# Output projections by seven quadrant products: two products accumulated in place, the additions into x in another order

## The reference, cut to what matters

```python
# first block, odd layer (retention), and second block, both layers
x = x + m_lat[2] * y_lat                  # y_lat = (gated retention output) @ odd_w_out,  2048 -> 1024
x = x + gt1 * (merged @ w_o[l])           # 1024 -> 1024, l = 0, 1
# behind each of them: norm, and a feed-forward
h = rms_norm_2(x, norm_ffn[l]) * (1.0 + sc2) + sh2
x = x + gt2 * ((silu(up_act) * up_lin) @ w_down[l])
```

## Time and profile before

| what | us |
|---|---|
| median of three runs | 2651.59 (2650.97 to 2651.84) |
| the profiled execution, its own time | 2649.23 |
| its span | 2647.4 |
| PE busy | 2549.9 (96%) |
| PE weight loads busy | 1940.2 (73%) |
| DVE busy | 1584.4 (60%) |
| ACT busy | 648.0 (24%) |
| granted TensorE clock, mean over the span | 0.996 |

### The profile page before, as it was taken

The page is one execution under the profiler, slowest core; times in us unless marked ns, Lnnn a source line. Parts: engine busy times, 40 slices in busy tenths (PEclk is TensorE's granted clock), DMA queues, the critical chain, the costliest instruction groups (busy, mean ns, idle before and its releaser), DMA issues.

```text
span 2647.4 us, 39241 instructions
## 1 busy us (share of the span) xinstructions
PE 2549.9 (96%) x15996; PEld 1940.2 (73%) x15996; DVE 1584.4 (60%) x3133; ACT 648.0 (24%) x1717; POOL 0.2 (0%) x4
## 2 busy tenths in 40 slices
PE   6999899999999999999999999999999999999999
PEld 2545557888887864599996845668997854667999
DVE  4856667655877543266664664447773764437785
ACT  3144412111002111122202152233321144232320
POOL 0000000000000000000000000000000000000000
PEclk9999999999999999999999999999999999999999
DMA  8531115555574684245643432134663433114563
GB/s 334 194 95 44 45 32 169 153 175 171 201 276 160 256 301 173 80 128 160 191 165 127 159 64 96 65 112 137 167 198 132 148 101 96 65 66 143 164 178 122
DMA packets 339375, 386.66 MB, mean 146 GB/s; under 512 B 11116, under 2 KB 272380, under 8 KB 326908
## 3 DMA queue, kind: packets, MB, share of 16 engines
q1 hardware_dynamic: 336460, 378.15, 44.3%
q10 hardware_dynamic: 2736, 6.01, 0.6%
HBM read 383.08 MB, written 1.05 MB: 145 GB/s over the span
## 4 chain that ended last, share of the span: by engine, by line
PE 76%; DVE 12%; DMA 5%; issue 4%; ACT 3%; SPq 0%; ACTq 0%; DVEq 0%
PE acc L865 28%; PE mx L865 12%; PE acc L916 9%; PE acc L904 7%; PE acc L930 6%; DMA mod_w<-in_w_ada 2%; DVE arena L2514 2%; DMA mod_w<-in_mod_w 2%; PE acc L1285 2%; PE acc L1234 1%; PE mx L1633 1%; DVE arena L3356 1%; DVE hT L2547 1%; PE mx L1095 1%; PE mx L1620 1%
## 5 line engine op out<-in xcount | busy, mean ns | idle before, releaser
L865 PE MATMUL acc<-arena 128*128 128x128 f32 (+1 forms) x2312 | 369.4, 302 | 3.5 <-DVE arena L3102 1.0
L865 PEld LDWEIGHTS acc<-arena 128*128 128x128 f32 x2312 | 321.9, 191 | 22.2 <-ACT gate L2184 1.4
L2514 DVE SCALAR_TENSOR_TENSOR arena<-mod_w,vcols,arena 128x2048 f32<-128x2048 f32 x98 | 228.4, 2348 | 71.7 <-DMA mod_w<-in_w_ada 58.2
L904 PE MATMUL acc<-ring,hT 128*128 128x512 f32 x576 | 251.2, 596 | 5.9 <-ACT hT L1935 4.6
L916 PE MATMUL acc<-hT,ring 128*128 128x256 f32 (+1 forms) x1024 | 249.7, 406 | 0.8 <-DVE arena L3134 0.8
L930 PE MATMUL acc<-ring,hT 128*128 128x512 f32 x512 | 247.6, 605 | 0.7 <-ACT hT L1967 0.7
L916 PEld LDWEIGHTS acc<-hT,ring 128*128 128x128 f32 x1024 | 194.0, 190 | 55.0 <-issue 32.1
L904 PEld LDWEIGHTS acc<-ring,hT 128*128 128x128 f32 x576 | 109.3, 191 | 144.4 <-issue 139.3
L865 PE MATMUL acc<-hT,ring 128*128 128x128 f32 (+1 forms) x1336 | 202.7, 301 | 3.9 <-ACT hT L1935 1.7
L2878 DVE TENSOR_TENSOR arena<-ring 128x512 f32<-128x512 f32 (+1 forms) x136 | 91.7, 674 | 191.0 <-PE acc L865 182.1
L865 PE MATMUL acc<-arena,ring 128*128 128x128 f32 (+1 forms) x1288 | 199.0, 297 | 2.3 <-DVE x L2935 1.7
(11 more groups left out here) (433 smaller groups left out, 3414.4 us busy)
## 6 DMA issues: line engine op xcount, KB each, us to landing
ring<-in_w_in SPq DMA_DIRECT2D x28, 2048.0 KB
mod_w<-in_w_ada SPq DMA_DIRECT2D x48, 1024.0 KB, 5.3
ring<-in_ffn_w_in SPq DMA_DIRECT2D x88, 512.0 KB
ring<-in_w_up SPq DMA_DIRECT2D x88, 512.0 KB
mod_w<-in_mod_w SPq DMA_DIRECT2D x40, 1024.0 KB, 4.9
ring<-in_odd_w_in SPq DMA_DIRECT2D x12, 2048.0 KB
ring<-in_ffn_w_out SPq DMA_DIRECT2D x16, 1024.0 KB
ring<-in_w_down SPq DMA_DIRECT2D x16, 1024.0 KB
```

The source lines that it names most:

```text
L865: ins = nc.tensor.matmul(out, w[:, k, :], h[:, k, :], start=start and k == 0, stop=stop and k == n - 1, skip_group_check=more)
L904: ins = nc.tensor.matmul(b[:, 0:width], src[:, k, P * i:P * (i + 1)], w[:, k, :], start=k == 0, stop=k == KD - 1)
L2514: ins = V.scalar_tensor_tensor(acc_, mod_w[:, i % 2, :], vcols[:, at:at + 1], acc_, ALU.mult, ALU.add)
```

## The change

In the three projections, product 2 is accumulated onto product 1's bank once ACT has copied product 1 out, and product 3 onto product 5's bank once DVE has added product 5 into `x`. PE's order in a pair becomes 1, 4, 2, 5, 6, 7, 3. Products 1 and 5 alternate between two banks by pair. DVE runs a new function `quadrant_added` with seven gated additions and two sums a pair in place of nine and two. In `added_to_x`, which the feed-forwards keep, two additions into quadrant (1, 0) stand ahead of u3; the counts that PE and ACT wait for are renumbered to the new places. In `w_o` three of the four weight sums of pair 1 move from behind the fourth merge job to behind the third; of the first four weight sums of the feed-forward one stays ahead of the additions of pair 3, and three go behind them, ahead of `scaled_x`.

```diff
-WHERE = {1: 6, 2: 4, 4: 3, 5: 0, 6: 5, 7: 1, 3: 2}
+WHERE = {1: (6, 0), 4: (3, 3), 5: (4, 2), 6: (5, 5), 7: (1, 1)}
...
+                    t, e, d, first = tile.n, 28 * u + 7 * (p - 1), 28 * u + 7 * p, p == 0
...
+                    if p >= 2:
+                        pe.wait_ge(out_e, e - 7 + 2)
                     product(where[1], a_[0][0], b_[0][0], True, True, evens if first else lambda k: None).then_inc(out_d, 1)
 
-                    if p:
+                    if first:
+                        odds(pairs - 1)
+                    else:
                         pe.wait_ge(out_e, e + 1)
-                    product(where[2], a_[0][1], b_[1][0], True, True, odds if first else lambda k: None).then_inc(out_d, 1)
-
                     pe.wait_ge(out_ws, 4 * u + p + 1)
-                    if p:
-                        pe.wait_ge(out_e, e + 2)
                     product(where[4], s4, b_[1][1], True, True).then_inc(out_d, 1)
+
+                    pe.wait_ge(out_dt, 4 * u + p + 1)
+                    product(where[1], a_[0][1], b_[1][0], False, True, more=True).then_inc(out_d, 1)
...
                     if first:
                         pe.wait_ge(out_ts, 4 * u + 4)
-                    else:
-                        pe.wait_ge(out_e, e + 7)
-                    product(where[3], a_[1][1], t4, True, True).then_inc(out_d, 1)
+                    pe.wait_ge(out_e, d + 3)
+                    product(where[5], a_[1][1], t4, False, True, more=True).then_inc(out_d, 1)
```

In `added_to_x` (the old order of its tail was u3, (0,1), (1,1), (1,0) with product 5, (1,0) with u2, (1,0) with product 3):

```diff
                 V.tensor_tensor(u2, where[6], t1, ALU.add).then_inc(sem_e, 1)
-                dve.wait_ge(sem_e, e + 3)
+                gated(1, 0, where[5]).then_inc(sem_e, 1)
+                dve.wait_ge(sem_e, e + 4)
+                link(gated(1, 0, u2))
                 dve.wait_ge(full, d + 6)
                 V.tensor_tensor(u3, where[7], u2, ALU.add).then_inc(sem_e, 1)
-                dve.wait_ge(sem_e, e + 4)
+                dve.wait_ge(sem_e, e + 5)
                 gated(0, 1, u3).then_inc(sem_e, 1)
                 gated(1, 1, u3)
-                gated(1, 0, where[5]).then_inc(sem_e, 1)
-                dve.wait_ge(sem_e, e + 6)
-                link(gated(1, 0, u2))
                 dve.wait_ge(full, d + 7)
                 gated(1, 0, where[3]).then_inc(sem_e, 1)
```

In the merge loop and the call for `w_o`:

```diff
-                    if n >= 2:
-                        out_weights_summed("w_o", n - 2, 4)
+                    if n == 2:
+                        out_weights_summed("w_o", 0, 4)
+                        out_weights_summed("w_o", 1, 4, (0, 1, 2))
+                out_weights_summed("w_o", 1, 4, (3,))
                 job_done("mergeT", KD)
                 quadrants("w_o", 4 + 2 * l, hT[:, :, 0:256], 4, 2,
-                          lambda: weights_summed((KF + 12) * (2 + l), pl.tile[f"up@{l}"], 4))
+                          lambda: weights_summed((KF + 12) * (2 + l), pl.tile[f"up@{l}"], 4, (0,)),
+                          lambda: weights_summed((KF + 12) * (2 + l), pl.tile[f"up@{l}"], 4, (1, 2, 3)))
```

More of the change, by code:

```diff
@@ L958, in quadrants @@
                 b_, (t2, t3, t4) = out_blocks(src), out_input_sums(pairs)
-                where = {n: seven(WHERE[n], P) for n in WHERE}
                 stage(name)
                 for p in range(4):
-                    t, e, first = tile.n, 28 * u + 7 * (p - 1), p == 0
+                    where = {n: seven(WHERE[n][p % 2], P) for n in WHERE}
+                    t, e, d, first = tile.n, 28 * u + 7 * (p - 1), 28 * u + 7 * p, p == 0
                     if pairs == 8:
@@ L991, in quadrants @@
                     else:
-                        pe.wait_ge(out_e, e + 3)
+                        pe.wait_ge(out_e, e + 4)
                     product(where[6], s2, t2, True, True).then_inc(out_d, 1)
                     if p:
-                        pe.wait_ge(out_e, e + 4)
+                        pe.wait_ge(out_e, e + 5)
                     product(where[7], s3, t3, True, True).then_inc(out_d, 1)
@@ L1471, in seven_products @@
                         if p:
-                            pe.wait_ge(st_e, before + 6)
+                            pe.wait_ge(st_e, before + 4)
                         else:
@@ L1491, in seven_products @@
                         if p:
-                            pe.wait_ge(st_e, before + 4)
+                            pe.wait_ge(st_e, before + 5)
                         else:
@@ L2217, in ready @@
                         if p:
-                            act.wait_ge(out_e, 28 * u + 7 * p - 4)
-                        nc.scalar.activation(out_temps(pairs)[0], seven(WHERE[1], P), ACT.Copy).then_inc(out_dt, 1)
-                    act.wait_ge(out_e, 28 * u + 7 * p + (7 if block % 2 else 5))
+                            act.wait_ge(out_e, 28 * u + 7 * p - 3)
+                        nc.scalar.activation(out_temps(pairs)[0], seven(WHERE[1][p % 2], P), ACT.Copy).then_inc(out_dt, 1)
+                    act.wait_ge(out_e, 28 * u + 7 * p + (7 if block % 2 else 6))
                 return ready
@@ L2239, in down0_done @@
                         mod_turn()
-                act.wait_ge(st_e, 7 * p + (7 if block % 2 else 5))
+                act.wait_ge(st_e, 7 * p + (7 if block % 2 else 6))
             squares(2, both, down0_done)
@@ L2864, in _, with weights_summed @@
                     residual_part(PARTS.index(slot - 1))
-            def weights_summed(n, tile, pairs):
+            def weights_summed(n, tile, pairs, only=(0, 1, 2, 3)):
                 s2, s3, s4 = weight_sums(n, pairs)
                 f, m = divmod(n, KF + 12)
[L2869 to L2875, removed]
+                if 0 in only:
+                    if m >= 2:
+                        kind, count = ("down" if pl.released[tile - 2][0] == "down" else "part", pl.released[tile - 2][1])
+                        if m < KF + 2:
+                            dve.wait_ge(st_x, KF * f + m - 1)
+                        else:
+                            dve.wait_ge(st_d if kind == "down" else w_part, count)
+                    dve.wait_ge(h_in[tile % (2 * RING)], pl.landed[tile][1])
                 w = half_tile(tile, 2 * pairs)
                 a00, a01, a10, a11 = (w[:, :, e, P * i:P * (i + 1)] for i in range(2) for e in range(2))
[L2878 to L2881, removed]
+                if 0 in only:
+                    V.tensor_tensor(s3, a11, a10, ALU.subtract)
+                if 1 in only:
+                    link(V.tensor_tensor(a10, a10, a00, ALU.subtract))
+                if 2 in only:
+                    link(V.tensor_tensor(s2, a11, a10, ALU.subtract))
+                if 3 in only:
+                    V.tensor_tensor(s4, a01, s2, ALU.subtract).then_inc(st_ws, 1)
             def out_weights_summed(name, p, pairs, only=(0, 1, 2, 3)):
@@ L2961, in added_to_x, with gated, quadrants @@
                         add_square(use + 1, block, width)
-            def quadrants(name, use, src, pairs, summed, early):
-                u, where = OUT_USE[name_of(name)], {n: seven(WHERE[n], P) for n in WHERE}
+            def quadrant_added(use, p, where, temps, d, n):
+                t1, u2, u3 = temps
+                first, m = 16 + 24 * (use % 2), mb[:, use // 2 % 2]
+                def gated(i, t, y):
+                    at = x[:, 1, 2 * p + i, P * t:P * (t + 1)]
+                    return V.scalar_tensor_tensor(at, y, m[:, 0, first + 2 * p + i:first + 2 * p + i + 1], at, ALU.mult, ALU.add)
+                dve.wait_ge(out_d, d + 2)
[13 more added lines that the diff above has]
+                gated(0, 1, u3).then_inc(out_e, 1)
+                gated(1, 1, u3)
+                dve.wait_ge(out_d, d + 7)
+                gated(1, 0, where[5]).then_inc(out_e, 1)
+                for block in (2 * p, 2 * p + 1):
+                    if 0 < block < KD - 1:
+                        add_square(use + 1, block, 256)
+            def quadrants(name, use, src, pairs, summed, early, late=None):
+                u = OUT_USE[name_of(name)]
                 inputs_summed(4 * u, out_blocks(src), out_input_sums(pairs), summed=out_ts)
@@ L2971, in quadrants @@
                         early()
-                    added_to_x(use, 256, p, where, out_temps(pairs), (out_d, 28 * u + 7 * p), (out_dt, 4 * u + p),
-                               (out_e, 28 * u + 7 * p))
+                    quadrant_added(use, p, {n: seven(WHERE[n][p % 2], P) for n in WHERE}, out_temps(pairs),
+                                   28 * u + 7 * p, 4 * u + p)
+                if late:
+                    late()
                 scaled_x(use + 1, 256)
```

9 lines of the change are left out of this document (4 added, 5 removed).

## The result

| | median us | runs | lowest to highest |
|---|---|---|---|
| before | 2650.74 | 11 | 2648.19 to 2652.06 |
| changed | 2658.39 | 11 | 2654.60 to 2660.91 |

The ratio is 1.0028, with a 95% interval of 1.0019 to 1.0037: the changed kernel is slower by 7.4 us (7.65 between the medians). The forecast was +3.4 and "within 0.2%"; the result is beyond that line by a little, outside the 2651 to 2656.9 that the forecast took for itself, inside the whole range (by 0.1 us), and beside rival B's 2659.2. The profiled execution took 2655.66 (span 2653.9, mean granted clock 0.997), 6.4 more than that of before.

What follows compares the result with a forecast made beforehand. The prediction took PE as the bound (76% of the chain, DVE 12%). w_o -5.07, ret_out +7.76 and down projections -1.11 gave +1.6; one clock fall, +1.8, made +3.4, so 2655.0 us, range 2648.0 to 2658.5.

Steps and rivals of the forecast that it cites:

- rival B: ret_out: the clock falls after both stalls, 3.0 us each, +7.6 in all, 2659.2 us; chance 0.14.
- `w_o`, the tail: End of w_o: DVE no longer late, scaling 3.19 us after the last product; gains 2.66 and 3.67 us.
- The start: w_o, pair 0: third product waits for ACT's copy of product 1, +0.63 us in each layer.
- Pairs 1 and 2, moved sums: w_o: the new wait for DVE's third addition and the weight sums moved ahead of the merge job cost 0.
- `ret_out`, the stall: ret_out: product 3 waits for DVE's third addition by 1.11, 3.26 and 3.39 us in pairs 0 to 2, +7.76.
- The clock: ret_out: two stalls may each bring half clock at about even chance; one fall taken, +1.8 us.
- Rivals A and C: A: PE doesn't stall in ret_out, -6.2 us, chance 0.12. C: DVE remains the bound in w_o, +6.0 us, 0.08.
- Down projections: Last addition of the kernel 0.77 us earlier, 0.17 less in each of two middle ones; sum -1.11 us.

Runs made afterwards that it cites:

- experiment 7: Changed kernel with DVE's first three additions ahead of the next pair's weight sums in ret_out, and ACT's table load ahead of mergeT's copies: 0.9974 of before, 2643.79 us.
- experiment 4: Changed kernel plus three 128x512 constant matmuls into an unused bank ahead of the wait in pairs 1 and 2 of ret_out: 1.0016 of before, 2655.61 us.
- experiment 2: Changed kernel with DVE's first three additions of a pair in ret_out ahead of the next pair's weight sums: 0.9983 of before, 2647.75 us.
- experiment 9: The changed kernel itself, profiled once more: one run, 2657.07 us.
- experiment 1: Changed kernel with ret_out back on seven banks and the old order of products: 0.9976 of before, 2645.08 us.
- experiment 6: Kernel before with only added_to_x's new order of additions, all projections on seven banks in the old order of products: 0.9985 of before, 2646.63 us.

## Why the prediction was nearly right

**`w_o`, the tail: right.** Scaling 3.19 after the last product was predicted; measured 1814.62 - (1810.59 + 0.89) = 3.14. The three late weight sums are hidden by 0.19, as the scaling still waits for ACT; the clock doesn't fall. **The start: right.** 1.53 - 0.89 = 0.64 against 0.63, and experiment 7 shows the cause. **Pairs 1 and 2, moved sums: right**, no wait shows. Together -1.92 - 2.92 = -4.84 in the stages, against -5.07.

**`ret_out`, the stall: right in place and cause, 0.9 too small.** Without a fall of the clock (experiment 4) the delays are 1.20, 3.58, 3.80 and 0.10, 8.68 in all against 7.76. The 0.9 comes in every pair. I took the additions' place from the old rows and let PE go on at full pace, but the product after a wait starts with an instruction longer than in a dense run (2.02 or 2.05 against 1.95), and since the tile's load is released by product 3, that tenth enters the loop again, once a pair. The rest is the load: from the end of product 3 to the first weight sum it took 7.99 in pair 1 and 8.11 in pair 2 before (the first from 1138.79 + 1.95 to 1148.73), and 8.23 and 8.43 in experiment 4. Why it took longer is open. Experiment 2 shows the cause: with the additions ahead of the sums the term is 0.

**The clock: the step that was mis-sized.** "Two stalls at about even chance: I take one, +1.8". Of eight long waits in four executions seven were followed by 0.50, so two falls are usual. That is rival B's mechanism. Its price of 3.0 a fall was too high, however: against the 8.68 without a fall, one fall cost 1.5 and two cost 2.8, 2.2 and 4.1, 1.1 to 2.0 each. So B's mechanism held while its sum, which comes within 1 us of the median, owes that partly to luck: too much for the clock stands against 0.9 too little for the loop and 1 to 2 us outside the stages (below). Nor was it more than luck that the median stayed inside the range: four of the eleven runs lie above its end at 2658.5. Slow products behind product 3 of pair 1 cost nothing, because pair 2 waits anyway: its idle is 3.23 in experiment 9, where product 3 alone was slow, and 2.15 in the first profile, where the next one took 2.97. Only product 3 itself lies in the loop; after the second fall the slow products of pair 3 count too, for that pair has no wait to absorb them.

**Rivals A and C: refuted.** PE stands in three pairs of `ret_out`, and in `w_o` neither an addition of pairs 1 and 2 nor a late sum holds anything up. A's gain of 6.2 is what the rest of the change is worth without the stall: 6.4 in experiment 1, 4.5 (2.1 to 6.9) in experiment 2.

**Down projections: right in kind, smaller.** -0.54 at the end instead of -0.77. The last addition did move by 0.77 against u3, as forecast: it starts 0.86 behind it and not 1.63. But u3 itself now starts 0.50 after the start of product 3 instead of 0.27, because the two additions into (1, 0) stand ahead of it; that takes 0.23 back, and the prediction left it out. The rows, before and after:

```profile
2641.53 0.29 DVE L2950 TENSOR_TENSOR hT<-acc,hT 128x128 f32<-128x128 f32 x1 [0.45 <-PE acc L865]
2648.77 0.29 DVE L2958 TENSOR_TENSOR hT<-acc,hT 128x128 f32<-128x128 f32 x1
2649.63 0.34 DVE L2941 SCALAR_TENSOR_TENSOR x<-acc,mb,x 128x128 f32<-128x128 f32 x1
```

The 0.17 waits in the two middle ones are gone.

**The sum.** The retention stage takes 363.85, 365.10 and 363.99 in the three profiles of the changed kernel, 10.8 to 12.1 more than before. So -4.84 - 0.54 + 10.8 to 12.1 = +5.5 to +6.7. Between the profiled executions themselves (2655.66, 2657.07 and 2657.04 against 2649.23) it is +6.4, +7.8 and +7.8, and between the medians +7.65: 1 to 2 us lie outside these stages. Feed-forward 1 holds 1.35, 1.28 and 1.58 of them. In the first of the three PE waited there for its first down tile (0.53) and for the sums on it (0.93). But the kernel with `ret_out` as before shows the same (215.73), and so does the one with `w_o` alone changed (215.93), while the one with `ret_out` as before and the table moved doesn't (214.40). So this varies between executions, and no run here says how often in which kernel, nor whether the change has a part in it. The filler kernel has 217.14. The stretch from the kernel's first scaling to its second varies too, and within one kernel: 362.83, 364.39 and 365.16 in the three profiles of the changed one, 364.57 in that of before. Both are open.

## What to carry to other kernels

When an accumulation goes onto a bank that was just read, the wait moves from "a pair later" to "the same pair", and everything that stands in the reader's list ahead of that read can move onto the path. Put the read first, and the work for the next tile behind it: that order was worth about 11 us here, and with it accumulating onto the read bank cost nothing in `ret_out` that these runs can tell. In `w_o` the same holds for ACT: a table load ahead of its copy cost 0.6 to 0.7 us a layer until it was moved. Before adding a wait, follow it once around: if the waiting work itself frees the buffer whose load stands ahead of the wait, the period becomes the sum of the loop (16.3 instead of 12.5 here).

## What the runs showed of the hardware that I hadn't expected

How long PE stood doesn't alone decide whether the clock falls. It fell to about 0.50 after idles of 3.55, 3.53, 3.47, 3.46, 3.23, 3.19 and 2.38 us, and not after 2.15, nor after 3.59 in the kernel before. In the kernel of experiment 6 the idle of 2.50 in layer 0 was followed by it (four filler matmuls in 3.35 instead of 1.88), the idle of 2.50 in layer 1 was not:

```profile
2423.06 0.67 PE L1136 MATMUL acc<-gate,fconst 128*128 128x256 f32 x2 [2.50 <-DVE gate L2594]
...
2424.00 1.88 PE L1129 MATMUL mx<-fconst 128*128 128x512 f32 x4
```

Three matmuls ahead of the wait kept it at 1.00 in both pairs where they stood. The Trainium skill ("TensorE: Matmul & The Clock Gate", Part 1) says that the throttled state is the default and that activity lifts it; the stretch of 0.50 in the changed kernel, which ends while PE works, agrees.
